# The axial stage's query norm factor: square root and reciprocal, or logarithm, exponential and one Newton step

## The chip, the core and the metric

The kernel runs on one core of a Trainium2 chip. Its engines work side by side, each through its own list of instructions, and meet at semaphores: TensorE (PE) multiplies matrices into the PSUM banks, VectorE (DVE) and ScalarE (ACT) work elementwise, GpSimd (POOL) splits weights, SyncE (SP) issues the transfers. The metric is the device time of one execution in microseconds; lower is better.

## The reference

Two transformer layers of one kind (block-sparse, differential, dilated and latent attention, convolutional feed-forward) are followed by two layers of a second kind. The change touches only the first branch of the mixer in the second kind, attention with a norm of every query head and a two-axis rotation, over 512 tokens, 8 query heads and 2 key heads of 64 numbers:

```python
def rmsnorm_2(x, g):
    xf = x.astype(jnp.float32)
    y = xf * lax.rsqrt(jnp.mean(xf * xf, axis=-1, keepdims=True) + EPS)
    return (y * g.astype(jnp.float32)).astype(x.dtype)

def global_axial_attention(q, k, v, gq, gk):
    ...
    q = rmsnorm_2(q.reshape(B, S, A_HEADS, HEAD_DIM), gq)
    k = rmsnorm_2(k.reshape(B, S, A_KV_HEADS, HEAD_DIM), gk)
    q = rope_2d(q, row, col) * (HEAD_DIM ** -0.5)
    k = rope_2d(k, row, col)
    ...
        s = jnp.einsum('bqkgd,bskd->bkgqs', qi, k).astype(jnp.float32)
        p = jax.nn.softmax(s, axis=-1)
        return jnp.einsum('bkgqs,bskd->bqkgd', p.astype(v.dtype), v)
```

The factor in question is the `rsqrt` of the mean square of each query head, one number for each token and head. EPS is 1e-6.

## The kernel before

Activations lie as 8 tiles of 128 features x 512 tokens. Each weight matrix arrives in blocks through two buffers, POOL splits it in a high and a low part, and PE makes every projection from three matmuls (high x high, high x low, low x high; lines 461 to 463) into bank PA or PB. The order on each engine is that of the code; nothing is reordered at run time. The last part of the program is a loop over the two layers of the second kind (`LAYERS2`), so each place below occurs in two passes.

In a pass the axial stage comes after the key and value projection and the pooling branch. It works in four groups of two query heads. A group has eight units: head 0 or 1 with one of four tiles of 128 queries. Unit t goes through these steps: PE multiplies queries and keys (line 667, two units at a time), DVE scales the scores and takes their minimum (1388), ACT takes the exponential with its row sum (1098), PE transposes it (595) two steps of t later, ACT copies the transpose to SBUF (1104), and PE forms the weighted sum of the values (708), both heads together, after that. Between these, at given t, PE runs parts of the next projection.

The queries of group g + 1 are prepared while group g runs, in what the code calls a turn, at t mod 8 = 3 to 7. DVE scales the projected queries by the layer norm (`scale_q`), ACT squares them and applies the gain (`q_square`, 1159 and 1164), PE sums the squares (`q_sum`, 778) into eight columns of PB (four query tiles x two heads) and rotates the queries (765), and DVE applies cosine and sine. The norm factor isn't multiplied into the queries: it is kept as 128x8 numbers in `rq_of` and applied to the scores in line 1388, one column a unit. ACT takes the square root of the eight columns of PB (`q_root`, 1172) at t mod 8 = 6 and thereby frees PB (`pb_taken`); DVE takes the reciprocal (1522) at t mod 8 = 7. So there are three turns in a pass, at t = 6, 14 and 22.

Group 0 has no group ahead of it. Its queries are prepared in `pool_tiles` on PE (`q_sum`, then `turn_rotate`, 786, which writes PB again and so waits for `pb_taken`), in the lines ahead of `attention` on ACT (1265, then `q_root`), and at the end of `pooling` on DVE (1769, the reciprocal 1772, then `turn`, 1566 and 1569).

ACT evaluates its functions out of tables, which are loaded in sets. The compiler puts an ACT_TABLE_LOAD ahead of an activation whose function isn't in the set loaded last; it shows under the activation's line. The square root is not in the set that is loaded for the exponential; copy and square need no load in either.

Of the kernel before, what the change touches and what calls it, by code (L numbers as in the profile page):

```python
# [8 lines left out]
ALU = mybir.AluOpType  # L9
ACT = mybir.ActivationFunctionType  # L10
# [6 lines left out]
EPS = 1e-6  # L17
# [42 lines left out]

def counts(kind, seg=None, fin=0, mix=0):
    c = dict(e=SEGMENTS[seg][0] if seg else 0, a=0, b=0, u=0, g=0, v=0, n=fin, f=0, k=0, s=0, q=0, h=0, x=0, z=0,
             m=0, d=0, r=0, xs=0, st=0, df=0, pl=0, dr=0, dc=0)
    if kind == "x_in":
        c.update(s=1 + DT, q=DT, h=DT)
    elif kind == "v":
        c.update(v=1, f=fin)
    elif kind == "q0":
        c.update(a=1, b=1)
    elif kind in ("causal", "na", "diff"):  # L70
        c.update(a=3, b=3, u=32, g=4, st=2 * STRIP_PARTS[kind], d=4 * UNIT_LINKS[kind], df=4 if kind == "diff" else 0,
                 dr=0 if kind == "diff" else 16, dc=0 if kind == "diff" else 4)
    elif kind == "axial":
        c.update(a=3, b=2 + 3, u=32, g=4, d=TURN_LINKS + UNIT_LINKS[kind], r=4, dr=16, dc=4)
    elif kind == "mla":
        c.update(a=8, b=8, u=16, g=4, d=4 * UNIT_LINKS[kind])
    elif kind == "mla_cq":
        c.update(a=1, b=1, f=fin)
    elif kind == "mla_kv":
        c.update(a=1, b=1, d=2)  # L80
    elif kind == "norm_small":
        c.update(d=1)
    elif kind == "norm_post":
        c.update(q=DT, h=DT, x=DT, d=DT)
    elif kind == "norm_final":
        c.update(q=DT, h=DT, x=DT)
    elif kind == "out":
        c.update(a=4, b=4, s=DT if mix else 1 + DT, q=DT, h=0 if mix else DT, xs=0 if mix else DT)
    elif kind == "up1":
        c.update(a=FT, b=FT, z=FT, k=1, d=1 + FT * 2)  # L90
    elif kind == "up2":
        c.update(a=FT, b=FT, z=FT, k=1, d=1 + FT * 5)
    elif kind == "merge":
        c.update(a=24, b=24, m=8, d=4 * 2)
    elif kind == "axial_kv":
        c.update(b=3, v=1, k=1, d=2 + TURN_LINKS, r=1)
    elif kind == "pool":
        c.update(a=5, pl=4, d=(1 + 2 + 3 + 4) + 4 * 2)
    c["w"] = 1 if kind == "v" else 0
    return c  # L100

UNIT_LINKS = {"causal": 0, "na": 2, "diff": 8 + 4 + 1 + 3, "axial": 3 * 3, "mla": 4 + 1}
TURN_LINKS = 2

SUM_STEP = 4
# [72 lines left out]
def build(nc, x_in, weights, consts, cols_in, lam_in, rel_in, rpb_in, strips_rel, strips_na, out):  # L180
    with ExitStack() as ctx:
# [3 lines left out]
        def sem(name):  # L185
            return ctx.enter_context(nc.semaphore(name))
# [60 lines left out]
        held = stats[:, 58:59], stats[:, 59:60]  # L247
        held_act = stats[:, 60:61]
        rden_of = rden, stats[:, 120:128]
        rq_root = stats[:, 100:108]  # L250
        rq_of = stats[:, 108:116], stats[:, 88:96]
        rsT = stats[:, 96:100]
        neglam = stats[:, 48:49]
# [49 lines left out]
        ax_sq, ax_ss, ax_n, ax_rot, ax_done = (sem(n) for n in ("ax_sq", "ax_ss", "ax_n", "ax_rot", "ax_done"))  # L303
        qn_ready, kn_ready, qr_ready, qr_raw, qr_rot, qr_done = (
            sem(n) for n in ("qn_ready", "kn_ready", "qr_ready", "qr_raw", "qr_rot", "qr_done"))
        kr_rot, kr_done = sem("kr_rot"), sem("kr_done")
        pool_f, pool_hi, pool_split, pool_out, pool_yhi = (
            sem(n) for n in ("pool_f", "pool_hi", "pool_split", "pool_out", "pool_yhi"))
        lam_dot, lam_exp, u_ready, u_done = sem("lam_dot"), sem("lam_exp"), sem("u_ready"), sem("u_done")
# [722 lines left out]
        def _(act):  # L1032
# [88 lines left out]
            def attention(b, kind, ytile, early=None, gain=None):  # L1121
                u, turns = b["u"], Y_TURN[kind]
                full = kind in ("na", "axial")
                scale = SUBG if kind == "diff" else 1.0
                act.wait_ge(o_taken, u + 2)
                for t in range(turns[3] + (2 if kind == "diff" else 4)):
                    if t == 4 and early is not None:
                        early()
                    if t < 32:
                        soften(u, t, S if full else (t // 2 % 4 + 1) * P)  # L1130
                    tt = t - 2
                    if 0 <= tt < 32:
                        copy_turned(u, tt, S if full else (tt // 2 % 4 + 1) * P)
                    if kind == "axial" and t < 24:
                        bn = axial_turn(b, t // 8 + 1)
                        if t % 8 == TURN["square"]:
                            q_square(bn["a"] + 2, gain)
                        if t % 8 == TURN["root"]:
                            q_root(bn["r"])
                    if kind == "diff" and t >= 12 and t % 8 == 4:  # L1140
                        g = (t - 12) // 8
                        act.wait_ge(yn_ss, 4 * b["df"] + 4 * g + 4)
                        A(rs4[:, 4:8], ss[:, 0:4], ACT.Sqrt, scale=1.0 / P, bias=eps[:, 0:1]).then_inc(yn_std, 1)
                    if t - 1 in turns:
                        g = turns.index(t - 1)
                        act.wait_ge(yt_ready, 2 * (b["g"] + g) + 3)
                        if kind == "diff":
                            A(tile(yh, ytile + g), (PB if g < 3 else O0)[:, :], ACT.Copy, scale=scale).then_inc(y_hi, 2)
                        else:
                            act.wait_ge(y_split, 2 * (b["g"] + max(g - 1, 0)) + 1)  # L1150
                            A(flat_y(g), (PB if g < 3 else O0)[:, :], ACT.Copy).then_inc(den_copied, 1)
                    if kind != "diff" and t - 3 in turns:
                        g = turns.index(t - 3)
                        act.wait_ge(o_taken, u + 8 * g + 8 + 2)
                        A(tile(yh, ytile + g), flat_y(g), ACT.Copy).then_inc(y_hi, 2)
# [11 lines left out]
                act.wait_ge(ax_ss, r_ + 1)  # L1167
                A(tmp[3][:, :], PB[:, :], ACT.Sqrt, scale=1.0 / 64, bias=eps[:, 0:1]).then_inc(pb_taken, 1)

            def q_root(r_):  # L1170
                act.wait_ge(ax_ss, r_ + 1)
                A(rq_root, PB[:, 0:8], ACT.Sqrt, scale=1.0 / 64, bias=eps[:, 0:1]).then_inc(pb_taken, 1)

            def mla(b):
                with act.Fori(0, 2) as i:
# [73 lines left out]
            with act.Fori(0, LAYERS2) as l:  # L1249
# [10 lines left out]
                for g, bank in enumerate((S0, S1, T0, T1)):  # L1260
                    if g < 3:
                        act.wait_ge(pool_out, 3 * l + g + 1)
                    else:
                        act.wait_ge(entry_done, b["e"] + 5 + 3)
                    A(yh[:, 4 + g, :], bank[:, :], ACT.Copy, scale=cols[:, bass.ds(CAT["pool_scale"] + l * CPER + g, 1)]
                      ).then_inc(pool_yhi, 1)
                q_root(ax["r"])
                attention(ax, "axial", 0, gain=gain)
                attention(H("na", l), "na", 8)
                merge(H("merge", l), l)  # L1270
# [8 lines left out]
        def _(dve):  # L1279
# [204 lines left out]
            def attention(b, kind, ytile, after=None):  # L1484
# [4 lines left out]
                arrived = lambda g: 16 * b["st"] + per_group * (g // 2 + 1)  # L1489
                ahead = lambda g: {**b, "e": b["e"] + 2 * g}  # L1490

                chain_at(b["d"] + (TURN_LINKS if kind == "axial" else 0))
                if kind == "na":
                    mask_strip(0, 0, arrived(0)); mask_strip(0, 1, arrived(0))
                for t in range(turns[3] + (3 if kind == "diff" else 5)):
# [16 lines left out]
                    if kind == "axial" and t < 24:  # L1512
# [5 lines left out]
                        if t % 8 == TURN["turn"]:  # L1518
                            q_turned(bn)
                        if t % 8 == TURN["invert"]:  # L1520
                            dve.wait_ge(pb_taken, bn["b"] + 2)
                            link(v.reciprocal(rq_of[(g + 1) % 2], rq_root))
                    elif t < 24 and t % 8 == Q_AT:
                        take_q(ahead(g), g + 1)
                    if kind != "axial" and t < 24 and t % 8 == K_AT:
# [33 lines left out]
            def q_cosine(r_):  # L1559
                dve.wait_ge(ax_n, r_ + 1)  # L1560
                link(STT(out=tmp[0][:, :], in0=turned_q, scalar=-0.125, in1=rope[:, 0, :], op0=ALU.mult, op1=ALU.mult))

            def turn(c, bb, r_, dst):

# [164 lines left out]
            def pooling(b, kv, ax, l):  # L1729
# [37 lines left out]
                for g, bank in enumerate((S0, S1, T0, T1)):  # L1767
                    dve.wait_ge(pool_yhi, b["pl"] + g + 1)
                    STT(out=yl[:, 4 + g, :], in0=bank[:, :], scalar=cols[:, bass.ds(CAT["pool_scale"] + l * CPER + g, 1)],
                        in1=yh[:, 4 + g, :].bitcast(F), op0=ALU.mult, op1=ALU.subtract)  # L1770
                dve.wait_ge(pb_taken, ax["b"] + 2)
                link(v.reciprocal(rq_of[0], rq_root))
                turn(-0.125, ax["b"], ax["r"], q_sb[:, :])


# [255 lines left out]
```

## Time and profile before

| | |
|---|---|
| median of 3 runs | 3167.78 us (3166.34 to 3168.57) |
| the profiled execution, whole | 3168.89 us |
| its span in the profile | 3167.1 us |
| busy of the span | PE 96%, POOL 52%, DVE 44%, ACT 25% |
| PE's share of the chain that ended last | 70% |
| TensorE's mean granted clock | 0.986 of full |

The profile is of one execution. Its span runs from the first instruction to the last; the time of the execution is 1.8 us longer. Busy time says how long an engine had work in hand; the idle time in front of an instruction carries in brackets how long the engine stood and which instruction's end released it. A granted clock of 1.00 is 2.4 GHz and one of 0.50 is 1.2 GHz.

### The profile page before, as it was taken

The page shows a single profiled execution, that of the slowest core. Times are in us where ns is not written, and L with a number is a line of the kernel's source. Part 1 is how long each engine was busy: PE and PEld are TensorE (multiplying, and loading weights), DVE is VectorE, ACT ScalarE, POOL GpSimd, SP SyncE. Part 2 cuts the span into 40 slices and gives each one's busy share as a digit, 9 for nine tenths or more (in the row PEclk, how much of TensorE's full clock was granted, in tenths as well). Part 3 has the DMA queues.
Part 4 walks back from the last instruction along what each step waited for, and adds up shares of the span by engine and source line. Part 5 has one row for each costly group of instructions (what it writes and reads, how often), then busy time and mean ns, then how long its engine had stood idle before and what let it go on. Part 6 is the DMA issues. An engine that isn't in the chain of part 4 may idle for free.

```text
span 3167.1 us, 44727 instructions
## 1 busy us (share of the span) xinstructions
PE 3039.9 (96%) x14812; PEld 2395.7 (76%) x14812; DVE 1400.9 (44%) x2439; ACT 795.7 (25%) x1437; POOL 1658.1 (52%) x1254
## 2 busy tenths in 40 slices
PE   8998999999899999989999999999889999999998
PEld 6777788886578888756678878888657688878886
DVE  3244544223445442352533476640734433576622
ACT  2333222112432220134421122210253411132211
POOL 4334666664146667423346656666323266646674
PEclk9999999999999999999999999999989999999999
DMA  6252223322022232211412222233112222223232
GB/s 160 77 152 75 91 95 106 104 86 89 26 67 93 96 109 100 73 41 52 102 61 96 84 75 96 99 104 103 48 41 71 71 90 99 84 73 99 93 115 77
DMA packets 99604, 274.90 MB, mean 87 GB/s; under 512 B 38127, under 2 KB 38895, under 8 KB 99491
## 3 DMA queue, kind: packets, MB, share of 16 engines
q1 hardware_dynamic: 97328, 269.07, 26.5%
q10 hardware_dynamic: 2162, 4.36, 0.7%
q8 instruction: 67, 1.10, 0.1%
q14 instruction: 47, 0.38, 0.0%
HBM read 269.66 MB, written 11.54 MB: 89 GB/s over the span
## 4 chain that ended last, share of the span: by engine, by line
PE 70%; DVE 3%; ACT 2%; issue 2%; DVEq 0%; ACTq 0%
PE PA L461 11%; PE PA L463 10%; PE PA L462 10%; PE PB L461 9%; PE PB L462 8%; PE PB L463 8%; PE O L708 2%; PE S L667 2%; PE T L595 2%; PE O L493 1%; DVE hl L1314 1%; DVE tmps L1353 0%; PE PB L725 0%; DVE strip L1741 0%; PE O L601 0%
## 5 line engine op out<-in xcount | busy, mean ns | idle before, releaser
L443 POOL TENSOR_TENSOR wl<-raw,wh 128x1024 fp32r<-128x1024 f32 (+2 forms) x416 | 1126.5, 2708 | 33.3
L440 POOL TENSOR_TENSOR zero<-zero 128x1 f32<-128x1 f32 x416 | 82.5, 198 | 1444.3 <-PE PA L463 713.8
L461 PE MATMUL PA<-hh,wh 128*128 128x512 f32 x1392 | 565.1, 406 | 27.2 <-DVE hl L1314 8.1
L463 PE MATMUL PA<-hh,wl 128*128 128x512 f32 x1392 | 549.6, 395 | 0.0
L462 PE MATMUL PA<-hl,wh 128*128 128x512 f32 x1392 | 549.3, 395 | 0.0
L441 POOL CAST wh<-raw 128x1024 fp32r<-128x1024 f32 (+2 forms) x416 | 475.0, 1142 | 0.0
L461 PEld LDWEIGHTS PA<-hh,wh 128*128 128x128 f32 x1392 | 266.2, 191 | 137.6 <-issue 67.0
L461 PE MATMUL PB<-hh,wh 128*128 128x512 f32 x896 | 357.9, 399 | 0.0
L463 PE MATMUL PB<-hh,wl 128*128 128x512 f32 x896 | 349.4, 390 | 0.0
L462 PE MATMUL PB<-hl,wh 128*128 128x512 f32 x896 | 349.2, 390 | 0.0
L463 PEld LDWEIGHTS PA<-hh,wl 128*128 128x128 f32 x1392 | 265.4, 191 | 56.7
L462 PEld LDWEIGHTS PA<-hl,wh 128*128 128x128 f32 x1392 | 266.2, 191 | 53.6 <-issue 1.5
L1098 ACT ACTIVATE probs<-biased,stats 128x512 f32<-128x512 f32 (+2 forms) x240 | 155.2, 646 | 381.9 <-PE T L595 252.8
L1670 DVE SCALAR_TENSOR_TENSOR tmps<-S,cols,tmps 128x511 f32<-128x511 f32 (+1 forms) x264 | 197.9, 750 | 39.4 <-DVE tmps L1670 20.0
L461 PEld LDWEIGHTS PB<-hh,wh 128*128 128x128 f32 x896 | 168.2, 188 | 47.8 <-issue 15.1
L463 PEld LDWEIGHTS PB<-hh,wl 128*128 128x128 f32 x896 | 168.3, 188 | 35.6
L462 PEld LDWEIGHTS PB<-hl,wh 128*128 128x128 f32 x896 | 168.3, 188 | 33.7 <-issue 1.2
L1190 ACT ACTIVATE T<-tmps 128x512 f32<-128x512 f32 x88 | 53.0, 602 | 393.3 <-DVE tmps L1670 393.3
L595 PEld LDWEIGHTS T<-ident,probs 128*128 128x128 f32 x792 | 96.4, 142 | 56.7 <-ACT probs L1098 21.5
L461 PE MATMUL PA<-acth,wh 128*128 128x512 f32 x352 | 137.4, 390 | 0.0
L1192 ACT ACTIVATE acth<-T 128x512 f32 x88 | 52.7, 599 | 336.7 <-DVE T L1697 336.7
L463 PE MATMUL PA<-acth,wl 128*128 128x512 f32 x352 | 137.0, 389 | 0.0
(303 smaller groups left out, 4809.1 us busy)
## 6 DMA issues: line engine op xcount, KB each, us to landing
raw<-in_w_up SPq DMA_DIRECT2D x176, 512.0 KB, 3.5
raw<-in_w_down SPq DMA_DIRECT2D x64, 768.0 KB, 4.2
raw<-in_w_merge SPq DMA_DIRECT2D x48, 768.0 KB, 4.2
raw<-in_w_out SPq DMA_DIRECT2D x32, 512.0 KB, 3.5
strips_na<-in_rpb SPq DMA_DIRECT2D x1, 7620.0 KB, 32.9
raw<-in_w_pool SPq DMA_DIRECT2D x12, 512.0 KB, 3.5
raw<-in_w_na_qk SPq DMA_DIRECT2D x12, 512.0 KB, 3.5
raw<-in_w_na_v SPq DMA_DIRECT2D x8, 512.0 KB, 3.4
```

The source lines that it names most:

```text
L440: nc.gpsimd.tensor_tensor(zero[:, :], zero[:, :], zero[:, :], ALU.add)
L441: nc.gpsimd.tensor_copy(wh[s][:, 0:width], raw[s][:, 0:width]).then_inc(w_head, 1)
L443: nc.gpsimd.tensor_tensor(wl[s][:, 0:width], raw[s][:, 0:width], wh[s][:, 0:width].bitcast(F), ALU.subtract).then_inc(w_split, 1)
L461: mm(dst, h_, rh, start=first, stop=False)
L462: mm(dst, h_, rl, start=False, stop=False)
L463: return mm(dst, l_, rh, start=False, stop=last)
L595: last = nc.tensor.transpose(TB[t % 2][:, k * P:k * P + P], probs[t % 2][:, k * P:k * P + P], ident[:, :])
L667: mm(SB[head][:, 0:span(t)], queries[g % 2][r, qt * P:qt * P + P], (axial_key if kind == "axial" else keys[g % 2])[r, 0:span(t)], start=Tr ...
L708: last = mm(bank[r, q], values(head, k), probsT[head][:, k * P:k * P + P], start=(k == 0), stop=(k == L // P - 1))
L1098: A(probs[t % 2][:, 0:L], biased[t % 2][:, 0:L], ACT.Exp, scale=-1.0, bias=mn[:, t % 8:t % 8 + 1], accum_out=den[:, t % 8:t % 8 + 1]).then ...
L1190: A(GELU[:, :], tmp[0][:, :], f).then_inc(gelu_ready, 1)
L1670: ins = STT(out=dst[:, lo:hi], in0=src[:, lo - d:hi - d], scalar=w(k), in1=dst[:, lo:hi], op0=ALU.mult, op1=ALU.add)
```

## The change

The factor is computed as exp(-0.5 ln(m + eps)), where m is the mean square, and then corrected once: y becomes y (1.5 - 0.5 (m + eps) y^2). ACT computes the logarithm out of PB and the exponential (`q_estimate`), in place of the root; DVE reads PB for m + eps (`rq_mean`) and takes three chained steps on 128x8 numbers (`q_factor`), in place of the reciprocal. PB is freed by DVE's reading and no longer by ACT's. A table set that holds both functions is loaded by name ahead of the first estimate of each pass. Counts of semaphores are adapted.

```diff
@@ counts
-        c.update(a=3, b=2 + 3, u=32, g=4, d=TURN_LINKS + UNIT_LINKS[kind], r=4, dr=16, dc=4)
+        c.update(a=3, b=2 + 3, u=32, g=4, d=TURN_LINKS + 2 + UNIT_LINKS[kind], r=4, rq=4, dr=16, dc=4)
...
-        rq_root = stats[:, 100:108]
+        rq_log, rq_mean, rq_step = stats[:, 100:108], tmps[:, 2, 0:8], tmps[:, 2, 8:16]
...
@@ ACT
                         if t % 8 == TURN["root"]:
-                            q_root(bn["r"])
+                            q_estimate(bn, bn["turn"])
...
-            def q_root(r_):
-                act.wait_ge(ax_ss, r_ + 1)
-                A(rq_root, PB[:, 0:8], ACT.Sqrt, scale=1.0 / 64, bias=eps[:, 0:1]).then_inc(pb_taken, 1)
+            def q_estimate(b, n):
+
+                act.wait_ge(ax_ss, b["r"] + 1)
+                A(rq_log, PB[:, 0:8], ACT.Ln, scale=1.0 / 64, bias=eps[:, 0:1]).then_inc(rq_logged, 1)
+                act.wait_ge(rq_logged, b["rq"] + n + 1)
+                A(rq_of[n % 2], rq_log, ACT.Exp, scale=-0.5).then_inc(rq_ready, 1)
...
-                q_root(ax["r"])
+                nc.scalar.preload_act_table_set("natural_log_exp_and_others")
+                q_estimate(ax, 0)
...
@@ DVE
-                            dve.wait_ge(pb_taken, bn["b"] + 2)
-                            link(v.reciprocal(rq_of[(g + 1) % 2], rq_root))
+                            q_factor(bn, g + 1)
...
+            def q_factor(b, n):
+
+                y = rq_of[n % 2]
+                dve.wait_ge(rq_ready, b["rq"] + n + 1)
+                TS(rq_mean, PB[:, 0:8], 1.0 / 64, EPS, ALU.mult, ALU.add).then_inc(pb_taken, 1)
+                dve.wait_ge(pb_taken, b["b"] + 2)
+                link(TT(rq_step, y, y, ALU.mult))
+                link(STT(out=rq_step, in0=rq_step, scalar=-0.5, in1=rq_mean, op0=ALU.mult, op1=ALU.mult))
+                link(STT(out=y, in0=rq_step, scalar=1.5, in1=y, op0=ALU.add, op1=ALU.mult))
...
-                dve.wait_ge(pb_taken, ax["b"] + 2)
-                link(v.reciprocal(rq_of[0], rq_root))
+                q_factor(ax, 0)
                 turn(-0.125, ax["b"], ax["r"], q_sb[:, :])
```

The changed file has a few more lines, so some of the numbers below differ by 3 or 4 (ACT's pooling copies stand in 1265 before and in 1268 now). PE's order and SP's are as before.

ACT at the start of the stage, before: the last two pooling copies, the root, and the first exponential with its load.

```order
L1265 ISA
L1265 ACTIVATE yh<-T,cols 128x512
L1264 ISA
L1265 ISA
L1265 ACTIVATE yh<-T,cols 128x512
L1171 REGISTER_ALU
L1172 ACTIVATE stats<-PB,eps 128x8
L1125 ISA
L1096 REGISTER_ALU
L1097 REGISTER_ALU
L1098 ACT_TABLE_LOAD
L1098 ACTIVATE probs,stats<-biased,stats 128x512
```

The same place in the changed kernel (1173 is the logarithm, 1175 the exponential of the estimate):

```order
L1268 ACTIVATE yh<-T,cols 128x512
L1267 ISA
L1268 ISA
L1268 ACTIVATE yh<-T,cols 128x512
L1270 ACT_TABLE_LOAD
L1172 REGISTER_ALU
L1173 ACTIVATE stats<-PB,eps 128x8
L1175 ACTIVATE stats<-stats 128x8
L1125 ISA
L1096 REGISTER_ALU
L1097 REGISTER_ALU
L1098 ACTIVATE probs,stats<-biased,stats 128x512
```

The load has moved from behind the factor to the place ahead of it, and one activation is added.

ACT at turn 2 (t = 14), before: the copy of a transpose, the root, the high part of y (1155), the next exponential and copy.

```order
L1104 ACTIVATE probsT<-T 128x512
L1171 REGISTER_ALU
L1172 ACT_TABLE_LOAD
L1172 ACTIVATE stats<-PB,eps 128x8
L1155 ACTIVATE yh<-y_tok 128x512
L1096 REGISTER_ALU
L1098 ACT_TABLE_LOAD
L1098 ACTIVATE probs,stats<-biased,stats 128x512
L1104 ACTIVATE probsT<-T 128x512
```

The same place in the changed kernel:

```order
L1104 ACTIVATE probsT<-T 128x512
L1172 REGISTER_ALU
L1173 ACTIVATE stats<-PB,eps 128x8
L1175 ACTIVATE stats<-stats 128x8
L1155 ACTIVATE yh<-y_tok 128x512
L1096 REGISTER_ALU
L1098 ACTIVATE probs,stats<-biased,stats 128x512
L1104 ACTIVATE probsT<-T 128x512
```

Both loads are gone and one activation is added; the rest keeps its order.

DVE at turn 2, before: the scaling of unit 15's scores, the inverse of a softmax sum (1424), the reciprocal, the low part of y and the scaling of unit 16's.

```order
L1388 TENSOR_SCALAR biased,stats<-S,stats 128x512
L1424 RECIPROCAL stats<-stats 128x2
L1521 REGISTER_ALU
L1522 RECIPROCAL stats<-stats 128x8
L1288 REGISTER_ALU
L1433 ISA
L1434 TENSOR_TENSOR yl<-y_tok,yh 128x512
L1383 REGISTER_ALU
L1388 TENSOR_SCALAR biased,stats<-S,stats 128x512
```

The same place in the changed kernel:

```order
L1392 TENSOR_SCALAR biased,stats<-S,stats 128x512
L1428 RECIPROCAL stats<-stats 128x2
L1570 TENSOR_SCALAR tmps<-PB 128x8
L1571 REGISTER_ALU
L1572 TENSOR_TENSOR tmps<-stats 128x8
L1292 REGISTER_ALU
L1573 SCALAR_TENSOR_TENSOR tmps<-tmps 128x8
L1292 REGISTER_ALU
L1574 SCALAR_TENSOR_TENSOR stats<-tmps,stats 128x8
L1292 REGISTER_ALU
L1437 ISA
L1438 TENSOR_TENSOR yl<-y_tok,yh 128x512
```

One instruction of 128x8 has become four, the first of which reads PB.

## Rows read from the trace of the kernel before

**Rows 1.** The page, part 1: busy us (share of the span) and instructions.
```profile
PE 3039.9 (96%) x14812; PEld 2395.7 (76%) x14812; DVE 1400.9 (44%) x2439; ACT 795.7 (25%) x1437; POOL 1658.1 (52%) x1254
```

**Rows 2.** Groups of ACT by line: count, busy us, mean ns, idle before.
```profile
L1098 ACT ACT_TABLE_LOAD x13 | 16.7, 1283 | 22.7 <-DVE biased L1388 11.9 <-DVE stats L1392 10.7
...
L1172 ACT ACT_TABLE_LOAD x6 | 7.7, 1283 | 0.1
```

**Rows 3.** Timeline, ACT, stage start: start us, us, instruction [idle before <-releaser].
```profile
1374.99 1.26 ACT L1265 ACTIVATE yh<-T,cols 128x512 fp32r<-128x512 f32 x2
1376.13 0.28 ACT L1172 ACTIVATE stats<-PB,eps 128x8 f32<-128x8 f32 x1
1382.35 1.28 ACT L1098 ACT_TABLE_LOAD   x1 [5.93 <-DVE biased L1388]
```

**Rows 4.** Timeline, PE, start of the stage.
```profile
1374.50 0.95 PE L778 MATMUL PB<-onesblk,tmps 128*128 128x2 f32 x8
1376.47 1.12 PE L786 MATMUL PB<-strip,perm 128*128 128x512 f32 x2 [1.02 <-ACT stats L1172]
1379.39 2.26 PE L667 MATMUL S<-kr_sb,q_sb 64*128 64x512 f32 x4 [1.79 <-DVE q_sb L1569]
```

**Rows 5.** Timeline, DVE, start of the stage.
```profile
1377.72 0.69 DVE L1566 SCALAR_TENSOR_TENSOR tmps<-PB,rope 128x512 f32<-128x512 f32 x1
```

**Rows 6.** Windows of one us, PE: length, busy (x), granted clock, DMA share, GB/s.
```profile
1378.00:1379.00 1.00, 0.00 (x0) 0.78 0.71 215
...
1385.00:1386.00 1.00, 1.00 (x5) 0.80 0.00 0
```

**Rows 7.** Timeline, ACT, turn 2 of the first pass.
```profile
1425.69 0.60 ACT L1104 ACTIVATE probsT<-T 128x512 f32<-128x512 f32 x1
1426.30 1.28 ACT L1172 ACT_TABLE_LOAD   x1
1427.60 0.27 ACT L1172 ACTIVATE stats<-PB,eps 128x8 f32<-128x8 f32 x1
...
1428.40 1.28 ACT L1098 ACT_TABLE_LOAD   x1
1429.70 0.72 ACT L1098 ACTIVATE probs<-biased,stats 128x512 f32<-128x512 f32 x1
...
1430.42 0.57 ACT L1104 ACTIVATE probsT<-T 128x512 f32<-128x512 f32 x1
```

**Rows 8.** Timeline, PE: weighted sums of turn 1, then turns 2 and 3 twice.
```profile
1406.00 1.09 PE L708 MATMUL O<-probsT,tmps 128*64 128x128 f32 x16
...
1431.05 1.09 PE L708 MATMUL O<-probsT,tmps 128*64 128x128 f32 x16 [0.38 <-ACT probsT L1104]
...
1457.74 1.09 PE L708 MATMUL O<-probsT,tmps 128*64 128x128 f32 x16 [1.06 <-ACT probsT L1104]
...
2354.50 1.09 PE L708 MATMUL O<-probsT,tmps 128*64 128x128 f32 x16 [0.85 <-ACT probsT L1104]
...
2382.55 1.09 PE L708 MATMUL O<-probsT,tmps 128*64 128x128 f32 x16 [1.07 <-ACT probsT L1104]
```

**Rows 9.** Timeline, DVE, turn 2 of the first pass.
```profile
1427.90 0.20 DVE L1522 RECIPROCAL stats<-stats 128x8 f32<-128x8 f32 x1 [1.04 <-ACT stats L1172]
```

**Rows 10.** Line 1745: count: ns min/median/max, first and last start, forms.
```profile
L1745 DVE TENSOR_TENSOR strip<-strip,edge x8: 166/168/2249, 1336.2 to 2291.3; 128x8 f32<-128x8 f32 x8
```

**Rows 11.** Line 1231, the same columns.
```profile
L1231 ACT ACTIVATE stats<-stats x1: 190/190/190, 21.3 to 21.3; 128x2 f32<-128x2 f32 x1
```

**Rows 12.** Windows of 10 us: busy us of PE, PEld, DVE, ACT, POOL; clock.
```profile
1440.00:1450.00 10.00, 7.57 (x46) 4.35 (x44) 2.89 (x7) 5.26 (x12) 1.19 (x1) 0.84 0.18 52
...
2338.00:2348.00 10.00, 7.57 (x46) 4.24 (x44) 3.88 (x10) 4.99 (x12) 0.00 (x0) 0.83 0.13 47
...
2368.00:2378.00 10.00, 8.99 (x43) 5.55 (x44) 3.82 (x7) 3.73 (x9) 0.00 (x0) 0.66 0.00 0
```

**Rows 13.** Waits of PE, first pass: us in total, times, longest us.
```profile
PE PB L778 <- ACT y_tok L1151: 4.9, 2, 2.4
```

More of the change, by code:

```diff
@@ L62, in counts @@
     c = dict(e=SEGMENTS[seg][0] if seg else 0, a=0, b=0, u=0, g=0, v=0, n=fin, f=0, k=0, s=0, q=0, h=0, x=0, z=0,
-             m=0, d=0, r=0, xs=0, st=0, df=0, pl=0, dr=0, dc=0)
+             m=0, d=0, r=0, rq=0, xs=0, st=0, df=0, pl=0, dr=0, dc=0)
     if kind == "x_in":
@@ L100, in counts @@
     return c
-UNIT_LINKS = {"causal": 0, "na": 2, "diff": 8 + 4 + 1 + 3, "axial": 3 * 3, "mla": 4 + 1}
+UNIT_LINKS = {"causal": 0, "na": 2, "diff": 8 + 4 + 1 + 3, "axial": 3 * 5, "mla": 4 + 1}
 TURN_LINKS = 2
@@ L305, in build @@
             sem(n) for n in ("qn_ready", "kn_ready", "qr_ready", "qr_raw", "qr_rot", "qr_done"))
-        kr_rot, kr_done = sem("kr_rot"), sem("kr_done")
+        kr_rot, kr_done, rq_logged, rq_ready = sem("kr_rot"), sem("kr_done"), sem("rq_logged"), sem("rq_ready")
         pool_f, pool_hi, pool_split, pool_out, pool_yhi = (
@@ L1490, in attention @@
                 ahead = lambda g: {**b, "e": b["e"] + 2 * g}
-                chain_at(b["d"] + (TURN_LINKS if kind == "axial" else 0))
+                chain_at(b["d"] + (TURN_LINKS + 2 if kind == "axial" else 0))
                 if kind == "na":
```

## The prediction

> **What bounds the kernel now.** I read the page first: TensorE (PE) is busy for 96% of the span, ScalarE (ACT) for 25% and VectorE (DVE) for 44% [rows 1]. Work taken off ACT or put on DVE therefore counts only where PE stands and waits for it, and the question is asked of the axial stage alone, from 1374 to 1470 us in the first pass of the layer loop and from 2296 to 2392 us in the second. Next I read the costliest groups of ACT: six table loads stand at the root of line 1172 and thirteen at the exponentials of line 1098 [rows 2]. Eight of the thirteen belong to the axial stage, one after each of the eight roots. The reader is to see that one load always takes 1.283 us, so the stage holds 14 loads or 18.0 us of ACT time, in both passes together. Then I read the timelines of the three engines at the two kinds of places that matter.
>
> *The start of the stage.* ACT ends its four copies of the pooling outputs at 1376.25 and starts the first root at 1376.13, with no load ahead of it [rows 3]. PE stands idle from 1375.45 for that root and rotates the queries at 1376.47 [rows 4]. Then come DVE's sine product at 1377.72 [rows 5] and its sum, and PE starts the first scores at 1379.39 after 1.79 us of idle [rows 4]. The first exponential's load, at 1382.35, comes after 5.93 us in which ACT had nothing to do [rows 3], and PE is kept busy meanwhile by the next query projection; it is off the path.
>
> *The three turns inside the attention.* In the second and third turn ACT runs a load, the root, the copy of y, another load, one exponential and then the copy that PE needs [rows 7]. PE is ready 0.38 us before that copy's end in the first pass at turn 2, 1.06 us at turn 3, and 0.85 and 1.07 us in the second pass; at turn 1 (1406.00) its row has no wait [rows 8].
>
> **The change part by part.**
>
> *Loads removed inside the stage.* Two at each of three turns, in two passes: 12 x 1.283 = 15.4 us of ACT time. On the path lies only what PE waits: 0.38 + 1.06 + 0.85 + 1.07 = 3.4 us [rows 8]. Is all of it won? At turn 2 the logarithm can start at 1426.30, where the load stood. A root takes 0.27 us [rows 7]; I take that for the logarithm. An exponential on two columns took 0.19 us [rows 11], a 128x8 form with its wait for the logarithm takes about 0.3. So 2.57 us go and 0.3 come, and the copy that began at 1430.42 begins at about 1428.1 and ends at 1428.7; PE is ready for it at 1431.05 - 0.38 = 1430.67 [rows 7, 8]. That leaves 2.0 us of slack, and at turn 3, where PE waits longest, 2.3 - 1.07 = 1.2 us. The whole 3.4 us is won, and what is late next is PE's own stream of matmuls. A gain of more than 3.4 can't come from here, and at turn 1 it is nothing.
>
> *Newton step on DVE.* One reciprocal becomes four instructions, three of them chained. A 128x8 product on DVE lasts 0.168 us; the longest of eight lasted 2.249 [rows 10]. DVE starts 0.03 us behind its releaser (the root ends at 1427.60 + 0.27, the reciprocal starts at 1427.90 [rows 7, 9]), so a link of the chain is 0.20. I take 0.8 us for the four against 0.20 for the reciprocal. At the turn DVE waits 1.04 us for the root today [rows 9], and the estimate is ready 1.0 us earlier than the root was, since the load ahead of it goes (1.28) and the exponential (0.3) comes. The four instructions then end some 0.4 us before the reciprocal ended. Cost 0. Behind the estimate's wait DVE has queued the low part of y and the scaling of the next scores; both move forward with it. The other end: one instruction of 2.249 us holds them back 1.7 us, which PE would see only where it has less slack than that (rival D).
>
> *The start.* This is where the change costs. The load that was hidden now stands before the first logarithm, straight behind the last copy at 1376.25, and two more instructions stand before PE may overwrite the bank: the exponential, and DVE's mean, since the bank is now released by DVE. Step by step: load 1376.26, logarithm 1377.55 (a load start to the next activation is 1.30 us [rows 7]), exponential 1377.85 to 1378.13, mean 1378.16 to 1378.36, rotation on PE at 1378.42 (0.06 behind its releaser, as now [rows 3, 4]). It was 1376.47: plus 1.95 us. The three chained instructions (0.6 us) run beside the rotation (1.12 us) and cost nothing, and DVE's own low parts of the pooling outputs are done by then. At full clock that is 1.95 us for each pass, 3.9 in all. PE has no slack to take it up: its projections follow at once.
>
> *The clock at the start.* PE's granted clock fell from full (2.4 GHz) to half (1.2 GHz) within the microsecond from 1378 and came back within that from 1385 [rows 6]. Ahead of the fall PE had stood idle for 1.02 us before the rotation and from its end on, 1.79 us in all [rows 4]. The rotation would now lie where the clock falls: at half clock its 1.12 us becomes 2.2 us (as the scores took 2.26 [rows 4]), so 0 to 1.1 more in each pass. Against that, if full clock comes back at the same moment as now although PE starts later, less of its work is done at half speed, and up to half of the delay is given back: 0 to 1.5 in each pass. Ends for the start over two passes: 2.0 (3.9 less half) and 6.1 (3.9 and 2 x 1.1). I take 1.9 for the rotations and 1.4 back, so 4.4 us, nearest to the rows as they stand.
>
> *A rule on the load's price.* In the rows a load begins 0.01 us after the copy ahead ends (1425.69 + 0.60, then 1426.30) and the next activation starts 1.30 us after it [rows 7]. The Trainium skill, "ScalarE: Activation LUTs", section "What ACT_TABLE_LOAD costs", gives the same 1283 ns and puts a drain of about 1380 ns beside it, 2.66 us for a switch. By that rule the start would cost 2 x 1.38 = 2.8 us more. The trace shows no such drain, so the sum goes by 1.30; the page's price is a rival below.
>
> **Sum.** -3.4 at the turns, +4.4 at the start: +1.0 us. The profiled execution took 3168.89 us for a span of 3167.1, so it would become 3169.9. The median of the runs shown is 1.1 us below it, 3167.78, which becomes 3168.8 us. I call the outcome no measurable change: 0.2% of this kernel is 6.3 us, and less than that its measurement can't tell.
>
> **The rivals.**
>
> *A: the turns lose their clock loss too.* Behind the long wait ahead of the query's sums PE's mean granted clock over 10 us is 0.84 once in the first pass and 0.83 and 0.66 in the second [rows 12]. With full or half clock as the only levels that makes stretches of 3.2, 3.4 and 6.8 us (twice the missing share of 10 us), each costing half its length, 6.7 us in all. With shorter waits some could vanish. All of them gone: 3167.8 + 1.0 - 6.7 = 3162.1 us. Against it: the waits that precede those stretches (at most 2.4 us, for ACT's copy of the denominators [rows 13]) are not among those that the change shortens. One stretch gone or added is 1.6 us either way, and that belongs to the range.
>
> *B: slower, by the start.* If PE, idle from 1375.45 almost without a break until 1381, keeps half clock for one more stretch of about 3.3 us in each pass, that costs 1.65 twice; with the full 6.1 us at the start and the turns' 3.4 back it gives +6.0, so 3173.8 us. It decides once the start costs more than 3.4 us beyond what the turns return. For it speaks that the clock falls exactly there now; against it, that it also returned within 6 us with the work that follows.
>
> *C: the load costs its drain, by rule.* The first logarithm comes later by a time that the rows bound at nothing but that a slow switch would give: each pass's start longer by one more load's length (1.3 us, so +2.6), 3171.4 us. This is the rule of the Trainium skill named above.
>
> *D: another wait takes the place of the four.* If at the turns something else on ACT or DVE (the copy of y, a 2.25 us DVE instruction) holds PE as long, only the start is left: 3167.8 + 4.4 = 3172.2 us. The 1.2 us of slack speak against it.
>
> *E: it doesn't do what it says.* If the loads stayed inside the loop of units, time would rise by the start and the exponentials. The order of instructions has none left there, so I give this nothing.
>
> **How the numbers follow.** The forecast (about +1, own range -2 to +4, 3165.8 to 3171.8) has 0.65, A in part or whole 0.12, B 0.08, C 0.05, D 0.10. The range that should hold 8 in 10 reaches to one or two stretches lost on the fast side and to B on the slow side: 3164.5 to 3173.5. Beyond 0.2% faster lies only a tail of A, 0.04; beyond 0.2% slower a tail of B joined with C, 0.05; within, 0.91.
>
> **What would show it.** In the changed profile: one load in each pass, straight behind the pooling copies, and none at line 1098 in the stage; PE's rotation about 2 us later behind the last pooling matmul than now; no wait of PE's weighted sums for the copy at turns 2 and 3; four DVE instructions of about 0.2 us a factor; exponentials of the scores no longer than 0.72 us out of the new table set. I am wrong if PE's waits at the turns stay, if the rotation comes less than 1.5 or more than 3 us later, or if the total moves by more than 5 us.

## The result, and the profile after

The changed kernel takes 3174.16 us (median of 20 runs, 3166.99 to 3177.89) beside 3168.94 us for the kernel before (20 runs). The ratio is 1.0015 with a 95% interval of 1.0009 to 1.0021: 4.8 us slower, 2.9 to 6.7. (The ratio is an estimate of its own and not that of the medians, which lie 5.2 us apart.) Forecast were 3168.8 us and a move of +1.0; the time lies outside the range of 3164.5 to 3173.5. The profiled execution is the slowest of the 20. It took 3177.89 us for a span of 3175.8, and PE's mean granted clock in it is 0.983, where it was 0.986.

The page's first part, beside [rows 1]:

```profile
PE 3046.0 (96%) x14812; PEld 2398.0 (76%) x14812; DVE 1408.9 (44%) x2463; ACT 780.9 (25%) x1433; POOL 1661.5 (52%) x1254
```

ACT is busy 15 us less, DVE 8 us more. ACT's groups with table loads in them (count, busy us, mean ns, idle before), beside [rows 2]:

```profile
L1098 ACT ACT_TABLE_LOAD x5 | 6.4, 1283 | 10.4 <-DVE stats L1396 10.4
...
L1270 ACT ACT_TABLE_LOAD x2 | 2.6, 1283 | 0.0
```

Of thirteen loads at line 1098 five are left, all outside the stage; the six at the root are gone; the two new ones, one a pass, are line 1270's. At the start of the stage, first pass, ACT's timeline (start us, length us, instruction) beside [rows 3]:

```profile
1376.49 1.26 ACT L1268 ACTIVATE yh<-T,cols 128x512 fp32r<-128x512 f32 x2
1377.77 1.28 ACT L1270 ACT_TABLE_LOAD   x1
1379.06 0.27 ACT L1173 ACTIVATE stats<-PB,eps 128x8 f32<-128x8 f32 x1
1379.36 0.21 ACT L1175 ACTIVATE stats<-stats 128x8 f32<-128x8 f32 x1
```

PE's, beside [rows 4]:

```profile
1376.00 0.95 PE L778 MATMUL PB<-onesblk,tmps 128*128 128x2 f32 x8
1379.82 1.37 PE L786 MATMUL PB<-strip,perm 128*128 128x512 f32 x2 [2.88 <-DVE tmps L1570]
1382.97 2.26 PE L667 MATMUL S<-kr_sb,q_sb 64*128 64x512 f32 x4 [1.78 <-DVE q_sb L1582]
```

And DVE's, beside [rows 5]:

```profile
1379.60 0.17 DVE L1570 TENSOR_SCALAR tmps<-PB 128x8 f32<-128x8 f32 x1 [0.52 <-ACT stats L1175]
1379.80 0.17 DVE L1572 TENSOR_TENSOR tmps<-stats 128x8 f32<-128x8 f32 x1
1380.00 0.17 DVE L1573 SCALAR_TENSOR_TENSOR tmps<-tmps 128x8 f32<-128x8 f32 x1
1380.20 0.17 DVE L1574 SCALAR_TENSOR_TENSOR stats<-tmps,stats 128x8 f32<-128x8 f32 x1
```

The load comes straight behind the last copy, the logarithm 1.29 us after the load's start, the exponential 0.30 us after the logarithm, the mean and three links 0.20 us apart. PE waits 2.88 us for the bank where it waited 1.02. From the load to the rotation it takes 2.05 us, forecast were 2.16: the sequence of the forecast to about 0.1 us. The three links end before the rotation does. Turn 2 of the first pass on ACT, beside [rows 7]:

```profile
1431.11 0.60 ACT L1104 ACTIVATE probsT<-T 128x512 f32<-128x512 f32 x1
1431.60 0.26 ACT L1173 ACTIVATE stats<-PB,eps 128x8 f32<-128x8 f32 x1
1431.90 0.21 ACT L1175 ACTIVATE stats<-stats 128x8 f32<-128x8 f32 x1
1432.01 0.61 ACT L1155 ACTIVATE yh<-y_tok 128x512 fp32r<-128x512 f32 x1
1432.53 0.70 ACT L1098 ACTIVATE probs<-biased,stats 128x512 f32<-128x512 f32 x1
1433.24 0.57 ACT L1104 ACTIVATE probsT<-T 128x512 f32<-128x512 f32 x1
```

From the end of the copy ahead to the start of the copy that PE needs it is now 1.5 us and was 4.1. PE's waits in the first pass (us in total, times, longest):

```profile
PE PB L778 <- ACT y_tok L1151: 4.9, 2, 2.4
PE PB L786 <- DVE tmps L1570: 2.9, 1, 2.9
PE S L667 <- DVE q_sb L1582: 1.8, 1, 1.8
PE PB L778 <- ACT tmps L1159: 1.2, 1, 1.2
PE O L708 <- ACT probsT L1104: 0.6, 1, 0.6
```

Of the waits of the weighted sums for ACT's copy, [rows 8], only one of 0.6 us at the first units is left, which was there before. So all the waits of the first pass moved as forecast. The time went elsewhere, into the granted clock. PE in windows of 20 us (length, busy and count, granted clock, DMA share, GB/s), in a further profile of the kernel before (h1 below):

```profile
1376.00:1396.00 20.00, 16.57 (x68) 0.83 0.15 41
1396.00:1416.00 20.00, 18.71 (x137) 1.00 0.11 39
1416.00:1436.00 20.00, 17.13 (x129) 1.00 0.08 27
1436.00:1456.00 20.00, 17.51 (x126) 0.91 0.17 53
```

In a further profile of the changed kernel (h2 below):

```profile
1376.00:1396.00 20.00, 15.45 (x49) 0.74 0.12 37
1396.00:1416.00 20.00, 18.21 (x108) 0.83 0.04 14
1416.00:1436.00 20.00, 17.52 (x119) 0.83 0.15 53
1436.00:1456.00 20.00, 17.57 (x129) 1.00 0.16 54
```

At the start 0.74 where it was 0.83, then 0.83 twice where the kernel before was granted full clock, and 1.00 in the last window, where it had 0.91. In the first pass the loss is in and around turns 1 and 2, where the kernel before has none. The profiles of the changed kernel aren't alike: in these four windows the one at the top of this section has 0.83, 0.91, 0.91 and 0.91.

### The profile page after: what moved, and what is told of

The parts are those of the page before. It is cut to its first block, busy times and chain, and to the rows that moved or that the text cites. A ratio compares the mean times of both kernels' runs of the same rounds, so it can differ in the third digit from the quotient of the medians.

```text
span 3175.8 us, 44763 instructions
## 1 busy us (share of the span) xinstructions
PE 3046.0 (96%) x14812; PEld 2398.0 (76%) x14812; DVE 1408.9 (44%) x2463; ACT 780.9 (25%) x1433; POOL 1661.5 (52%) x1254
## 4 chain that ended last, share of the span: by engine, by line
PE 70%; DVE 3%; issue 2%; ACT 1%; DVEq 0%; ACTq 0%
PE PA L461 11%; PE PA L462 10%; PE PA L463 10%; PE PB L461 9%; PE PB L463 8%; PE PB L462 8%; PE S L667 3%; PE O L708 2%; PE T L595 2%; PE O L493 1%; DVE hl L1318 1%; DVE strip L1754 0%; DVE tmps L1357 0%; PE PB L725 0%; PE O L601 0%
## 5 line engine op out<-in xcount | busy, mean ns | idle before, releaser
L462 PE MATMUL PA<-actl,wh 128*128 128x512 f32 x352 | 137.0, 389 | 0.0
```

The source lines that it names most:

```text
L462: mm(dst, h_, rl, start=False, stop=False)
```

## A measure for the stage

PE executes the same matmuls in the same order in both kernels, so two profiles can be laid side by side. I take the stage from its first query-sum matmul (778) to the last scores that read the same key buffer, in the attention that follows: about 220 us a pass. *Clock loss* is half the time that PE was busy within the stage while half clock was granted, *net* the stage without it. The numbers are worked out from the traces. Net isn't the time that the stage would take at full clock, since part of what half clock costs is hidden behind waits: with all idle places filled (g2) 12.3 us of loss are gone and the stage is 11.1 us shorter. Below the first two rows each value is of one profile. Both passes together, in us; "start" is the time from the query sums to the first scores, pass by pass.

| kernel (profile) | start | stage | clock loss | net |
|---|---|---|---|---|
| before, three profiles | 4.9, 4.9 | 443.5, 443.6, 443.5 | 12.3, 12.3, 12.3 | 431.2, 431.3, 431.2 |
| changed, four profiles | 7.0 to 7.6, 6.9 to 8.8 | 447.7, 446.5, 446.5, 448.3 | 16.1, 15.2, 15.2, 18.6 | 431.6, 431.3, 431.3, 429.7 |
| e2 root at start | 4.9, 6.7 | 441.0 | 12.2 | 428.8 |
| e3 estimate at start only | 7.1, 6.8 | 446.5 | 11.9 | 434.7 |
| e4 load early | 6.3, 6.1 | 441.6 | 12.0 | 429.6 |
| f1 before, start filled | 4.9, 4.9 | 437.0 | 5.1 | 431.9 |
| f2 changed, start filled | 6.7, 6.8 | 444.0 | 13.7 | 430.4 |
| f3 as e2, start filled | 4.9, 4.9 | 434.4 | 6.8 | 427.6 |
| f4 no Newton steps | 7.5, 7.0 | 446.5 | 15.2 | 431.3 |
| g1 before, delayed by 12 roots | 7.2, 6.9 | 446.6 | 11.9 | 434.8 |
| i1, i2: by 5 and by 20 roots | 5.7 and 9.0 | 444.6, 449.0 | 11.9, 11.2 | 432.7, 437.8 |
| g2 before, all filled | 4.9, 4.9 | 432.4 | 0.0 | 432.4 |
| g3 changed, all filled | 6.8, 6.8 | 432.9 | 0.0 | 432.9 |
| g4 as e2, all filled | 4.9, 4.9 | 429.1 | 0.0 | 429.1 |

The four profiled spans of the changed kernel are on average 4.0 us longer than the three of the kernel before, and their stages 3.7 us: nearly all of it lies in the stage.

The times of all experiments, against the kernel before on the same chip, ratio with its 95% interval (again not that of the medians) and in us of 3169:

| run | median us | ratio | us |
|---|---|---|---|
| e1 changed again | 3172.46 | 1.0012 [1.0003, 1.0021] | +3.8 |
| e2 | 3164.78 | 0.9990 [0.9981, 0.9999] | -3.2 |
| e3 | 3175.24 | 1.0021 [1.0012, 1.0030] | +6.7 |
| e4 | 3167.18 | 1.0002 [0.9993, 1.0011] | +0.6 |
| f1 | 3164.30 | 0.9984 [0.9975, 0.9993] | -5.1 |
| f2 | 3171.30 | 1.0011 [1.0002, 1.0020] | +3.5 |
| f3 | 3159.42 | 0.9972 [0.9962, 0.9983] | -8.9 |
| f4 | 3177.12 | 1.0025 [1.0014, 1.0035] | +7.9 |
| g1 | 3175.61 | 1.0016 [1.0007, 1.0025] | +5.1 |
| g2 | 3158.02 | 0.9961 [0.9947, 0.9976] | -12.4 |
| g3 | 3157.12 | 0.9957 [0.9943, 0.9970] | -13.6 |
| g4 | 3155.39 | 0.9953 [0.9939, 0.9968] | -14.9 |

## The experiments

Two theories to begin with. W: only the work on the path counts, as in the prediction's sum. C: the longer idle time at the start also costs granted clock.

**e1, the changed kernel again.**

> The changed kernel itself, beside the others on one chip. Theory W (only the work on the path counts: the start +2.0 us in each pass, the turns -3.4 us in all): +1 us against the kernel before, granted clock as before. Theory C (the longer idle time at the start also costs granted clock): +4 to +6 us, with a mean granted clock 0.001 to 0.003 lower than the kernel before has.

+3.8, with an interval of +1.0 to +6.7. The middle is close to C's +4, but W's +1 stands at the interval's edge. The result's 20 runs, with 2.9 to 6.7, exclude it.

**e2, root at the start, estimates at the turns.**

```diff
-                nc.scalar.preload_act_table_set("natural_log_exp_and_others")
-                q_estimate(ax, 0)
+                q_root(ax["r"])
+                nc.scalar.preload_act_table_set("natural_log_exp_and_others")
...
-                q_factor(ax, 0)
+                dve.wait_ge(pb_taken, ax["b"] + 2)
+                link(v.reciprocal(rq_of[0], rq_log))
```

> Group 0 keeps its root and reciprocal, and the table set is loaded behind them; the three turns use the estimate and the Newton step. Theory W: the turns' gain alone, -3.4 us against the kernel before. Theory C: the same -3.4 us, and 0 to 1.5 us more for clock at the turns, so -3 to -5; in both no wait of the weighted sums for the copy at turns 2 and 3 and a wait of 1.0 us ahead of the rotation. If the Newton step or the exponential held somebody at the turns, 0 or slower.

-3.2, with an interval of -6.0 to -0.3, and 2.4 less in the net of the stage. PE's waits in the first pass:

```profile
PE PB L786 <- ACT stats L1172: 1.0, 1, 1.0
PE O L708 <- ACT probsT L1104: 0.7, 2, 0.6
```

The rotation in the second pass:

```profile
2298.67 1.84 PE L786 MATMUL PB<-strip,perm 128*128 128x512 f32 x2 [2.03 <-ACT stats L1172]
```

It waited 2.03 us where the kernel before waits 1.02. With this 1.0 us taken out, the 2.4 become 3.4, the gain that was forecast for the turns. In the first pass no wait of PE at the turns is left that the exponential or the Newton step could have caused.

**e3, estimate at the start, roots at the turns** (the converse edit).

> The converse: group 0 uses the load, estimate and Newton step, the three turns keep root and reciprocal with their two loads each. Theory W: the start's cost alone, +4.0 us. Theory C: +6 to +9 us, with the clock lower. The wait ahead of the rotation is 2.9 us in both.

```profile
PE PB L786 <- DVE tmps L1575: 2.9, 1, 2.9
PE O L708 <- ACT probsT L1104: 2.5, 4, 1.1
```

+6.7 with an interval of +3.8 to +9.5. W's +4 stands just inside, C's +6 to +9 too. Its profile doesn't bear C out: the stage lost no more clock (11.9) than the kernel before (12.3), and became 3.0 us longer.

**e4, the load thirty microseconds earlier.**

```diff
                 turn_square(pb_taken, bk["b"] + 2); k_root(bk["r"])
+                nc.scalar.preload_act_table_set("natural_log_exp_and_others")
...
-                nc.scalar.preload_act_table_set("natural_log_exp_and_others")
                 q_estimate(ax, 0)
```

> The changed kernel with the table set loaded some 30 us earlier, behind the key's root, where ScalarE is idle. The wait ahead of the rotation falls from 2.9 to about 1.6 us. Theory W: -3.4 at the turns and +1.3 for the two starts, so -2.1 us against the kernel before and 2.6 us less than the changed kernel. Theory C: 4 to 7 us less than the changed kernel, since the idle time at the start is nearly that of before.

```profile
PE PB L786 <- DVE tmps L1570: 2.3, 1, 2.3
PE O L708 <- ACT probsT L1104: 0.7, 2, 0.6
```

The wait for the rotation fell to 2.3, not to 1.6: with the load gone DVE's low parts of the pooling outputs stand in front of its mean, as they stood in front of the reciprocal. The time is +0.6 [-2.2, +3.5], 3 us below the changed kernel (e1); W and C aren't told apart by it. Its runs fall in two groups, six at 3164.7 to 3167.2 and five at 3172.1 to 3172.4, so that its median is 2.1 us below the kernel before while the ratio lies above 1.

**f1, f2, f3, PE's idle time at the start filled.** Matmuls of the identity by a constant into a free bank, ahead of the rotation and behind it:

```diff
-                q_sum(ax["b"], ax["r"]); turn_rotate(ax["b"], ax["r"], turned_q)
+                q_sum(ax["b"], ax["r"])
+                filler((512, 512, 256))
+                turn_rotate(ax["b"], ax["r"], turned_q)
+                filler((512, 256))
```

(One filler of 384 columns ahead of the rotation in the kernels whose wait there is 1.02 us.)

> The kernel before with matmuls of the identity by a constant, into an unused bank, in PE's idle time at the start of each axial stage: 384 columns ahead of the rotation, 512 and 256 behind it. They fit into the idle time (1.02 and 1.79 us). Theory W (idle time counts as such, and clock is noise): 0 to +1 us against the kernel before. Theory C (the idle time costs granted clock): half clock is no longer granted from the rotation to the first projection, where it costs up to 3 us a pass now, so -2 to -6 us.

> The changed kernel with the same filling, 512, 512 and 256 columns ahead of the rotation (2.9 us idle) and 512 and 256 behind it. Theory W: about the changed kernel's time, within 1 us. Theory C: the clock loss that the longer idle time added goes too, so 5 to 9 us less than the changed kernel and 0 to 2 us more than the filled kernel before.

> Root and reciprocal for group 0, estimates at the turns, and the filling of the kernel before. Theory W: -3.4 us against the kernel before, as without filling. Theory C: -3.4 and the filling's gain, so -6 to -9 us.

f1 gained 5.1 and f3 8.9, as C says. f2 was to be 5 to 9 us below the changed kernel by C, and missed. It gained next to nothing: +3.5 beside +3.8 to +4.8. PE's start in f2, with the fillers (line 514) in it:

```profile
1371.76 0.95 PE L783 MATMUL PB<-onesblk,tmps 128*128 128x2 f32 x8
1372.57 2.40 PE L514 MATMUL O<-causal,ident 128*128 128x512 f32 x6
1375.59 1.12 PE L791 MATMUL PB<-strip,perm 128*128 128x512 f32 x2 [0.63 <-DVE tmps L1578]
1376.55 1.45 PE L514 MATMUL O<-causal,ident 128*128 128x512 f32 x4
1378.50 1.35 PE L672 MATMUL S<-kr_sb,q_sb 64*128 64x512 f32 x4 [0.49 <-DVE q_sb L1590]
```

The scores start at full clock, 1.35 instead of 2.26 us, and no clock is lost at the start. But windows of 20 us in the same profile:

```profile
1376.00:1396.00 20.00, 17.68 (x83) 0.92 0.12 34
1396.00:1416.00 20.00, 20.00 (x135) 0.91 0.12 40
1416.00:1436.00 20.00, 17.57 (x106) 0.83 0.04 15
1436.00:1456.00 20.00, 17.57 (x121) 0.83 0.15 52
```

Half clock is granted behind the start, at all three turns. So C falls in the form that I gave it: the loss isn't made where the idle time was added. A guess that is left is that the start's delay shifts the turns, and with them their own idle time (up to 2.4 us ahead of the query sums, [rows 13]), against the moments at which the clock is set. I call this P. No run here shows such moments.

**f4, no Newton steps** (the three `link` lines of `q_factor` left out; the factor is the bare estimate).

> The changed kernel without the three chained Newton instructions on VectorE (the mean is still read; the factor is the bare estimate). If they are hidden, as the prediction says, the changed kernel's time within 1 us; if they are on the path at the start or at the turns, 1.2 to 4.8 us less (0.6 us for each of 2 or 8 places).

Its median is the highest of all, so the expected time was missed; its stage is 446.5 us with net 431.3, exactly as in two profiles of the changed kernel. In the stage, then, the steps cost nothing. Why its runs lay 3 us above the changed kernel's isn't settled; the intervals overlap. The profile was taken in its fastest run (3169.82 us), so it doesn't show what the others lost.

**g1, the kernel before with a delay and nothing else.**

```diff
+                act.wait_ge(ax_ss, ax["r"] + 1)
+                for k in range(12):
+                    A(scratch[:, 8 * k:8 * k + 8], PB[:, 0:8], ACT.Sqrt, scale=1.0 / 64, bias=eps[:, 0:1])
                 q_root(ax["r"])
```

> The kernel before with twelve more 128x8 roots on ScalarE (into a scratch tile) ahead of the root at the start of each axial stage: a pure delay of about 2 us a pass in front of the rotation, with no other table load, no logarithm, no Newton step and the bank released by ScalarE as before. Theory W: +4 us. Theory C: +6 to +8 us, as the kernel with the estimate for group 0 alone (+6.7). If the load or the Newton step did harm beside the delay, clearly less than that kernel.

```profile
1379.45 1.50 PE L787 MATMUL PB<-strip,perm 128*128 128x512 f32 x2 [2.92 <-ACT stats L1173]
```

A wait of 2.92 us made of roots costs +5.1 [+2.2, +7.9], which holds W's +4 and C's +6 to +8 alike, and the stage comes out as in e3 to 0.1 us (446.6 and 446.5). Load, logarithm, Newton step and the bank's release by DVE do no harm in the stage beside their delay. Windows at turns 1 and 2 of its first pass:

```profile
1396.00:1416.00 20.00, 18.41 (x114) 0.91 0.07 21
1416.00:1436.00 20.00, 17.57 (x117) 0.83 0.14 47
```

So the delay alone puts half clock at these turns (e3 has the same two shares). It only moves it, though: of the stage's loss 7.6 us lie in the first pass and 4.2 in the second, where the kernel before has 4.7 and 7.6.

**g2, g3, g4, the idle time at the turns filled too.**

```diff
+                pe.wait_ge(pa_taken, b["a"] + 2)
+                for w in (512,) if b["turn"] == 1 else (512, 512):
+                    mm(PA[:, 0:w], ident[:, :], causal[:, 0:w], start=True, stop=True)
                 pe.wait_ge(den_copied, b["dc"] + b["turn"] - 1)
```

> The filled kernel before, with PE's idle time ahead of the query sums at the turns filled too (512 columns at turn 1, twice 512 at turns 2 and 3). Theory C: the half clock inside the stage goes, -2 to -6 us against the filled kernel before. Theory W: no change against it, or slower by what the fillers overrun.

> The changed kernel with all of these places filled. Here the granted clock is taken out of the comparison: theory C says that against the equally filled kernel before only the work is left, +0 to +2 us (it was +7 with the start alone filled). If the difference stays at +5 or more, the loss is not the clock's.

> Root and reciprocal for group 0, estimates at the turns, all places filled: -3.4 us against the equally filled kernel before by both theories, and the fastest of all so far (some -9 to -14 us against the kernel before).

With this no half clock is granted in the stage in any of the three; g3's windows:

```profile
1396.00:1416.00 20.00, 19.94 (x141) 1.00 0.11 31
1416.00:1436.00 20.00, 19.43 (x122) 1.00 0.06 24
1436.00:1456.00 20.00, 19.43 (x147) 1.00 0.17 54
```

And the changed kernel is as fast as the kernel before, both filled: -13.6 and -12.4. Each interval is 9 us wide, but the two can be compared with each other: the six runs of g3 average 3157.5 us and the five of g2 3157.9, with standard deviations of 2.2 and 1.4, so that a difference of 4.8 us would show. The stage is 432.9 beside 432.4 us: +3.8 at the two starts, -3.3 at the turns. That is W's sum with the clock left out, 3.9 less 3.4. What lies outside the stage isn't equal in these two profiles (27.7 us of clock loss in g3, 21.0 in g2). g4 has the lowest median found: 3155.39 us, 0.9953 [0.9939, 0.9968], faster than both unfilled kernels; its stage is 14.4 us shorter than the kernel before's, of which the estimates at the turns are 3.3 and the filling 11.1.

**h1 to h4, four more profiles, two of each kernel.**

> A further profile of the kernel before. Theory C: PE's granted half clock from the query sums to the last scores of the axial stage costs 3 us at each start and, over both passes, 5 to 7 us at the turns (6.6 in the first profile).

> A further profile of the changed kernel. Theory C: about the same 2.5 to 4 us at each start, but 8 to 10 us at the turns over both passes (10.1 and 8.4 in the two profiles so far), more of it in the first pass, and some at turn 1, where the kernel before has none. Theory W: no more there than the kernel before has.

> As the look at the kernel before ahead of it: theory C, 5 to 7 us of half-clock loss at the turns over both passes and none at turn 1.

> As the look at the changed kernel ahead of it: theory C, 8 to 10 us of half-clock loss at the turns over both passes, some of it at turn 1.

The kernel before repeats itself: the loss in the stage is 12.3 us in all three profiles, of which 5.7 lie at the starts (the first 22 us from the query sums) and 6.6 at the turns (all that follows). The changed kernel doesn't: 15.2 to 18.6, of which 5.0 to 6.8 at the starts and 10.1, 8.4, 8.4 and 13.5 at the turns. In each of its four profiles half clock is granted at turn 1 of the first pass, in none of the kernel before. With only four and three profiles, spread over the runs as they fell, this is the size of the effect and not its distribution.

**i1, i2, other lengths of the delay.** As g1, with five and with twenty roots.

> The kernel before with five more roots at the start of each stage instead of twelve: about 0.8 us of delay a pass. Theory I (each us of idle time at the start costs clock in proportion): the half-clock loss in the stage grows with the delay, by some 40% of what twelve roots add. Theory P (the delay only moves the turns' idle time against the moments at which the clock is set): loss at the turns near that of the kernel before or of the twelve roots, by no rule of proportion.

> The same with twenty more roots, about 3.3 us of delay a pass. Theory I: the loss in the stage is well over that of twelve roots, above 15 us over both passes. Theory P: it isn't in proportion, and the loss at the turns of the first pass can come back to that of the kernel before (1.7 us) although the delay is larger.

The loss in the stage is 11.9, 11.9 and 11.2 us for 5, 12 and 20 roots: it doesn't grow with the delay. Its place does change. With 20 roots the first pass has:

```profile
1376.00:1396.00 20.00, 16.40 (x66) 0.74 0.11 36
1396.00:1416.00 20.00, 18.79 (x134) 1.00 0.08 28
1416.00:1436.00 20.00, 16.79 (x110) 0.91 0.08 27
1436.00:1456.00 20.00, 17.46 (x131) 1.00 0.15 54
```

The start is deeper at half clock (0.74 where h1 has 0.83), turn 1 is free again, and one low stretch has moved from the third turn to the second. P's rival, I (clock is lost by the idle time itself, and so grows with the delay), had to give over 15 us with 20 roots and falls. P isn't contradicted, which is less than shown: two single profiles show that proportion fails, not what the rule is.

## Why the prediction was wrong

- *The loads in the stage:* right. Twelve are gone, two stand in front of the logarithm, and the switch costs 1.29 us from the load's start to the next activation. The drain that the Trainium skill adds in "ScalarE: Activation LUTs" (What ACT_TABLE_LOAD costs), rival C, isn't seen.
- *The turns' 3.4 us:* right. 3.2 by e2's time, with a wide interval, and 3.3 in the filled stages.
- *Newton step free:* right in the stage (f4's profile, 0.20 us a link). Rival D fell with PE's waits: only the 0.6 us of the first units is left.
- *The start at full clock, 3.9 us:* right. 1.88 us a pass in the filled kernels, and a wait of 2.88 us in seven of the eight starts that the changed kernel's profiles show. In the second pass of the changed kernel's first profile the wait was 3.9 instead of 2.9, since ACT's copies ended 1.8 us behind PE's query sums and not 0.8; in that pass DVE's low part of the last pooling group took 0.96 us instead of 0.69. I had not seen that this lag varies; e2's second pass, with its wait of 2.03, is the same.
- *The clock:* this is the step that failed. I put it at +0.5 us (+1.9 for rotations at half clock, 1.4 given back; the rotations in fact took 1.1 us more, over both passes), looked for it only at the start, and left the turns' stretches to the range as a coin that falls either way (rival A). Measured is +4.0 us in the stage over four profiles against three, of which +0.4 lies at the starts and +3.5 at the turns. The net moved by -0.3, where the forecast's work makes +0.5. With both kernels filled, so that the stage has no half clock left, the difference is gone, as far as eleven runs tell (g2, g3): that shows the clock as the cause. Rival B came nearest in size, at +6.0, with 0.08 and the wrong place: not one more stretch behind the start, but at turns that the forecast took as unchanged, since their waits are not among those that the change touches. They aren't longer; they stand elsewhere.
- A is refuted in its direction: shorter waits at turns 2 and 3 didn't spare the stretches (e2 loses 6.7 us at the turns, the kernel before 6.6).
- *The base and the resolution:* the forecast started from the median of 3 runs, 3167.78; that of 20 is 3168.94, which is 1.2 of the 5.4 us by which the median missed. And 20 runs of each kernel tell 4.8 us from nothing, where the forecast called anything below 6.3 us beyond the measurement.

What stays open: which arrangement of start and turns is granted more clock. The delay alone (e3 11.9 us, g1 11.9) loses no more clock in the stage than the kernel before (12.3), nor do the shorter turns alone (e2 12.2), nor both with a shorter delay (e4 12.0). Only where the full delay and the shorter turns stand together does the loss grow: 15.2 to 18.6 in the changed kernel, 15.2 in f4, 13.7 in f2, whose start is filled. All but the changed kernel and the kernel before are single profiles, and the times don't need such a joint effect: e2's -3.2 and e3's +6.7 (or g1's +5.1) add up to +3.5 (or +1.9), near the result's +4.8. The stage also isn't all of it: e3's time rose by 6.7 us and its stage by 3.0, and outside the stage its profile and g1's each hold 28.8 us of clock loss, those of the kernel before 22.5 to 26.3. Why isn't known.

## What to carry to other kernels

A change that makes one stall 2 us longer and others shorter on a nearly full TensorE moves every later idle stretch. Here that went with 4 us more clock loss, eight times the sum of the work (0.5 us): read from the windows how much half clock the stage of the change holds (12 us here) and let the range allow for part of it on both sides. Fill the short waits with matmuls into a free bank first; here it gave 12.4 us (g2), where the change at the turns gives 3.3, and it made the work measurable by itself. A set that holds both functions pays inside a loop of exponentials, where it spares loads; at a first use that lies on the path and needed no load, keep the old function and load the set behind it, as e2 does.

## What the runs showed that I had not expected

- Three profiles of the kernel before lose the same 12.3 us of clock in the stage, at the same places, though their starts lie up to 3.4 us apart; what differs between them is lost outside it (22.5 to 26.3 us).
- One or two filler matmuls a place took the whole loss of 12.3 us away (g2) and shortened the stage by 11.1, at no cost to the start behind them: the time from query sums to first scores stayed at 4.89 us.
